# Prepared table panels in the first FFN: two panels rounded in one call, against one panel per call, three stages apart, and a catch-up call

## The reference, cut to what matters

```
def swiglu(x, w_up, w_down):
    g, u = jnp.split(x @ w_up, 2, axis=-1)
    return (jax.nn.silu(g) * u) @ w_down
...
for l in range(DEPTH):
    n = rmsnorm(h, P['norm_g'][l, 0]) * (1 + sc0) + s0
    h = h + 0.5 * g0 * swiglu(n, w_ffn_up[l, 0], w_ffn_down[l, 0])
    ...token mixing, with cosine and sine tables for the long transforms...
    h = h + 0.5 * g2 * swiglu(n, w_ffn_up[l, 1], w_ffn_down[l, 1])
```

## Time and profile before

| | us |
|---|---|
| median of 3 runs | 3406.59 |
| lowest and highest | 3404.95 to 3410.38 |
| the profiled execution | 3412.7 |
| its span in the trace | 3410.9 |

### The profile page before, as it was taken

One profiled execution on the slowest core, in us unless ns is written; L12 is line 12 of the kernel. 1 busy time (PEld: TensorE's weight loads), 2 busy tenths in 40 slices (PEclk: granted clock), 3 DMA queues, 4 the chain that ended last, 5 costly groups with the idle time before them and its releaser, 6 DMA issues.

```text
span 3410.9 us, 48527 instructions
## 1 busy us (share of the span) xinstructions
PE 3164.7 (93%) x20832; PEld 3086.8 (90%) x20832; DVE 1763.8 (52%) x2928; ACT 987.1 (29%) x1498; POOL 45.0 (1%) x87
## 2 busy tenths in 40 slices
PE   2877989998899999999999999999889999999998
PEld 1877989988799999999999999998789899999998
DVE  6533655654655565534356556565465546543334
ACT  2221212322344433212133121233234443322222
POOL 0000000000000000000000000000000000000000
PEclk9988999998999999999999999999899999999999
DMA  5333333242512252322223233333432134222222
GB/s 231 136 148 142 142 148 142 96 181 115 192 70 80 92 219 88 113 97 109 97 93 112 111 149 136 142 141 147 171 140 80 69 117 177 105 106 75 75 75 69
DMA packets 71831, 420.31 MB, mean 123 GB/s; under 512 B 8321, under 2 KB 10689, under 8 KB 39617
## 3 DMA queue, kind: packets, MB, share of 16 engines
q1 hardware_dynamic: 58176, 325.08, 25.8%
q0 software_dynamic: 8880, 52.57, 4.0%
q10 hardware_dynamic: 4560, 39.56, 2.9%
HBM read 365.63 MB, written 51.54 MB: 122 GB/s over the span
## 4 chain that ended last, share of the span: by engine, by line
PE 74%; DVE 12%; DMA 5%; ACT 5%; issue 4%; DVEq 0%; ACTq 0%; SPq 0%
PE tile_psum L511 35%; PE tile_psum L518 18%; PE tile_psum L802 4%; PE tile_psum L437 2%; PE tile_psum L472 2%; PE tile_psum L806 2%; ACT whi L1023 2%; PE misc_psum L437 2%; PE tile_psum L724 2%; PE tile_psum L664 2%; DVE wlo L1426 1%; PE misc_psum L724 1%; PE tile_psum L477 1%; DVE scaled L1525 1%; DMA raw<-in_w_proj 1%
## 5 line engine op out<-in xcount | busy, mean ns | idle before, releaser
L511 PE MATMUL tile_psum<-n_hi,whi 128*128 128x320 f32 x3264 | 753.3, 312 | 42.4 <-DVE hidden L1627 33.3
L511 PE MATMUL tile_psum<-n_lo,whi 128*128 128x320 f32 x3264 | 748.9, 310 | 0.0
L1426 DVE TENSOR_TENSOR wlo<-raw,whi 128x2048 fp32r<-128x2048 f32 (+2 forms) x202 | 444.4, 2201 | 337.2 <-ACT whi L1023 335.2
L511 PEld LDWEIGHTS tile_psum<-n_hi,whi 128*128 128x128 f32 x3264 | 553.3, 190 | 46.9 <-DVE hidden L1627 34.6
L511 PEld LDWEIGHTS tile_psum<-n_lo,whi 128*128 128x128 f32 x3264 | 553.8, 190 | 0.0
L1023 ACT ACTIVATE whi<-raw 128x2048 fp32r<-128x2048 f32 (+2 forms) x202 | 370.5, 1836 | 508.1 <-DMA raw<-in_w_up 253.7
L518 PE MATMUL tile_psum<-n_hi,wlo 128*128 128x320 f32 x3264 | 512.1, 308 | 0.0
L518 PEld LDWEIGHTS tile_psum<-n_hi,wlo 128*128 128x128 f32 x3264 | 486.8, 187 | 0.0
L511 PE MATMUL tile_psum<-x_hi,whi 128*128 128x320 f32 x1408 | 329.1, 315 | 37.3 <-DVE h L1572 31.1
L511 PE MATMUL tile_psum<-x_lo,whi 128*128 128x320 f32 x1408 | 326.7, 313 | 0.0
L511 PEld LDWEIGHTS tile_psum<-x_hi,whi 128*128 128x128 f32 x1408 | 242.7, 193 | 38.9 <-DVE h L1572 32.4
(11 more groups left out here) (273 smaller groups left out, 3894.5 us busy)
## 6 DMA issues: line engine op xcount, KB each, us to landing
raw<-in_w_up SPq DMA_DIRECT2D x88, 1024.0 KB, 4.8
w_ada<-in_w_ada SPq DMA_DIRECT2D x128, 512.0 KB, 5.6
raw<-in_w_down SPq DMA_DIRECT2D x32, 1024.0 KB, 4.8
raw<-in_w_gate SPq DMA_DIRECT2D x24, 1024.0 KB, 5.0
whi<-table_keep SPq DMA_DIRECT2D x20, 1024.0 KB, 4.8
wlo<-table_keep SPq DMA_DIRECT2D x20, 1024.0 KB, 7.0
g_keep<-gate_out POOLq DMA_DIRECT2D x48, 320.0 KB, 2.5
gates<-g_keep POOLq DMA_DIRECT2D x16, 960.0 KB, 7.5
```

The costliest lines, as they stand in the source:

```text
L511: pe.matmul(tps[:, t.s, m, 0:TH], blk(p, m * n + k)[0], (hi, lo)[b][:, k, tok], start=k == 0 and b == 0, stop=False)
L1426: dve.tensor_tensor(wlo[:, r, 0:cols], raw[:, r, 0:cols], whi[:, r, 0:cols].bitcast(F32), ALU.subtract)\
```

## The change

The six prepared panels stand after panels 5, 8, 11, 14, 17 and 20 of the layer, instead of 4, 6, 8, 10, 12 and 22. A call that meets a prepared panel now handles it alone, so each following panel is handled one call later than before. In the second half of stages 6, 9, 12, 15, 18 and 21 (`CATCH_UP`) ACT and DVE make one more call. Counted with the calls ahead of the FFN, 36 calls and 6 catch-ups meet 42 panels; before, 36 calls met 6 prepared panels and with them 6 more.

```diff
-PREPARED = {4: 0, 6: 1, 8: 2, 10: 3, 12: 4, 22: 5}
+PREPARED = {5: 0, 8: 1, 11: 2, 14: 3, 17: 4, 20: 5}
+CATCH_UP = [p + 1 for p in PREPARED]
@@ scalar engine, round_panel
                     act.activation(whi[:, r, 0:cols], raw[:, r, 0:cols], ACT.Copy).then_inc(hi_ready, 1)
-                    if KINDS[p] == "prepare":
+
+            stage = [0]
+
+            def catch_up(j):
+
+                if j == 1:
+                    if stage[0] in CATCH_UP:
                         round_panel()
+                    stage[0] += 1
@@ scalar engine, into_h
                     if j == 0:
                         round_panel()
+                    catch_up(j)
```

## The result

| | before | after |
|---|---|---|
| median, us | 3406.73 | 3303.74 |
| lowest and highest | 3404.95 to 3410.38 | 3298.23 to 3309.05 |
| runs | 4 | 4 |
| span of the trace | 3410.9 | 3296.4 |

The ratio is 0.9696, with a 95% interval of 0.9678 to 0.9714: 3.0% less time.

A forecast was written before the change was run, and what follows sets the result against it. Call order was taken as the bound: twelve PE waits in layer 0's first FFN. Idle 76.1 plus low clock 30.6 gives 106.7 us; 3412.7 less that is 3306.0 profiled, 6.1 above the median, so 3299.9 us, range 3295 to 3320.

The forecast's parts named there:

- The case that was forecast: Layer 0's first FFN: all twelve PE waits go, median 3299.9 us, lying at 3295 to 3305; chance 0.72.
- The bound: Layer 0's first FFN, stages 4 to 13, 22 and 23: call order costs 106.7 us, not DMA or engine width.
- no call asks for a panel whose slot PE is still reading: New panel sequence: every call comes at least one half stage, 7.04 us, after its load's issue, so the waits go.
- The sum: Twelve stages take 275.65 us, undisturbed 168.96; the difference, 106.7 us, comes off the profiled 3412.7.
- Idle and clock: The twelve stages' 106.7 us split into 76.1 us of PE idle and 30.6 us of PE busy at low clock.
- What is late next: Stages with later calls and catch-ups: rounding, splits, ada tiles and queues checked for new PE waits; cost nothing.
- Stage 3's `hidden`: Stage 3, thinnest place: DVE's `hidden` ends at 138.1, PE needs the tile at 138.8; cover 0.7 us, no cost taken.
- a cover of 2.8 us: After the catch-up in stage 12, 15 or 18: the next stage's second-half tile is free at 25.3, needed at 28.16.
- The load beside the copies: All six pairs of prepared-panel copies now fall together with a weight load, which takes 8.35 us; costs nothing.
- The bound of 12.1 us: Panel 6, rounded one call later: its load may land up to 12.1 us after issue before PE waits.
- one full wait per prepared panel: Rival, chance 0.09: loads beside copies take over 12.1 us, six times, at 8.9 us each, 53 us: 3353.
- The price of one wait: One PE wait in layer 0's first FFN with its clock loss: mean 106.7 / 12 = 8.9 us, used for rivals.

## Why the prediction was right

**Forecast 3299.9, range 3295 to 3320, measured 3303.7.** The case that was forecast came in: all twelve waits went, and 3.1% was forecast where 3.0% was measured.

**The bound.** Order of the calls and not DMA or an engine: shown. The calls alone give the whole gain, and the places alone give none and cost some microseconds. The DMA share even rises to 0.52 without a wait. The step "no call asks for a panel whose slot PE is still reading" decides in all seven arrangements that were run (these two, and five of the experiments): it says how many waits there are, and in which stages.

**The sum.** 106.7 us were worked out, 106.3 lie between the two traces at the mixer's first load. Between the medians it is 103.0 us. The missing 3 us are no more than the 4.1 us by which the start of the mixer differs between traces; no run shows where they lie. The prediction's range had this only as the spread of the kernel before.

**Idle and clock.** The split into 76.1 us of idle time and 30.6 us at the low clock is right as a reading: with PE kept busy in the waits the clock is at 0.97 to 1.00. It is not a sum of independent parts. With the waits filled the stages won 22.5 us of clock, but loads that took longer gave 9.2 back, and 10 us are left by the medians.

**What is late next.** Nothing, as forecast. Stage 3's `hidden` could be checked against layer 1 beforehand, and PE didn't wait. For stage 13 a cover of 2.8 us was worked out; in the kernel after (DVE's timeline, stage 13) the row is

```profile
277.03 0.49 DVE L1645 TENSOR_TENSOR hidden<-gate_act,tile_psum 128x320 f32<-128x320 f32 x1
```

with the first half of stage 12 ended at 251.87 (ACT's SiLU starts there), so the tile is free at t = 25.65 instead of 25.3, and 2.5 us are left.

**The load beside the copies.** Forecast 8.35 us for all six. Where ACT waits for it, so that the landing can be seen, it is 7.0, 4.75 and 7.7 us:

```profile
195.49 1.92 ACT L1024 ACTIVATE whi<-raw 128x2048 fp32r<-128x2048 f32 x1 [4.63 <-DMA raw<-in_w_down]
...
235.49 1.91 ACT L1024 ACTIVATE whi<-raw 128x2048 fp32r<-128x2048 f32 x1 [11.22 <-DMA raw<-in_w_up]
...
365.20 1.91 ACT L1024 ACTIVATE whi<-raw 128x2048 fp32r<-128x2048 f32 x1 [3.05 <-DMA raw<-in_w_down]
```

(issued at 188.50, 230.74 and 357.46). So 8.35 was on the high side. It was not all six either: P2 is rounded in a down stage, as soon as it lands, so its second copy went out 3.4 us ahead of the load (227.34), which took what a load takes alone.

The bound of 12.1 us is where the low part of the panel is late. With two ada tiles the tile is late first: in the run with doubled copies a load that landed after 11.4 us held PE up for 0.44, so the bound there was 11.0. It changed nothing at 7.7.

Wrong was the reason that I gave for why it could not be more. I had read the Trainium skill ("DMA: Bandwidth & Descriptors", section on queues, rings and completion order: turns between queue rows, packet by packet) as equal shares of the bytes from the load's issue on, and estimated 9.5 us at worst. The trace agrees with turns once both queues move (0.88 MB against 0.70 in four microseconds), but not from the issue on: ahead of that SP's queue moved nothing for five microseconds, and the load took 12.0 us. The measurement decides. So the rival "one full wait per prepared panel" was argued down with a wrong reason; with 2 MB more of copies the load already stands at the bound.

**The price of one wait.** For the rivals I used the mean, 106.7 / 12 = 8.9 us. That is the step that was mis-sized: 8.7 us with one ada tile (52.3 / 6) and 11.1 us with two (66.5 / 6). It did not enter the forecast, as all waits went. The rival of six full waits would have had a price of 52 to 66 us, by the stages, instead of 53, if a wait behind a late load costs what one behind a late call does; no run shows that.

## What to carry to other kernels

When engines work through their lists in order, ask of every helper call which transfer it waits for and which event lets that transfer start; if the event is later than the call, everything behind the call on that engine waits too, and moving the call can be enough. Here it gave 103 us with not one instruction added or removed. Work that is put between others at the cost of a buffer shortens the look-ahead, so its neighbours have to be called later, too. And price a wait as a chain of its parts, since a mean hides which stage it was taken from.

## What the runs showed of the hardware

A 1 MB load on SP's queue mostly landed 4.7 to 4.9 us after its issue when no copy was near, some up to 5.8. Three loads of the kernel with filled waits took 6.3 to 6.4 us, with no cause found. With two copies of 1 MB on POOL's queue issued around it, the second at most 1.5 us before or after it, it took 6.9 to 8.4 us. With four it took 10.1 to 12.0 us.

In the case of 12.0 us SP's queue moved nothing in the first five microseconds, while POOL's moved 1.81 MB; in the next four it moved 0.88 MB and POOL's 0.70. The distance to the copies counts: 3.4 us behind the second one a load took 4.75 us, 2.8 us behind it 5.75, 1.0 to 1.1 us behind it 6.9 to 8.3, and 0.5 us behind it 7.7 to 8.1.

A wait of 4.7 to 5.7 us was enough for the granted clock to fall to the lower level (1.2 instead of 2.4 GHz), at 2.2 to 2.6 us for each wait. Of the waits left over by the filling, the first matmuls behind those of 0.2 to 2.7 us were at the higher level, and behind those of 3.5 and 4.2 us at the lower one.
